# Six norms between blocks: the end of one block and the beginning of the next run by token block, and the norm weight is multiplied in before the transpose

## The reference

```
for l in 0, 1:
    h  = rms_norm(x, g_mix[l])                  # norm "mix", l
    x += merged(branches(h @ w_in[l])) @ w_merge[l]
    h2 = rms_norm(x, g_ffn[l])                  # norm "ffn", l
    x += (silu(conv3(h2 @ w_gate[l])) * (h2 @ w_up[l])) @ w_down[l]
for l in 0, 1:
    h  = rms_norm(x, norm_w_2[l])               # norm "two", l
    x += concat(mla, gated delta rule, block attention)(h @ w_in_2[l]) @ w_out_2[l]
out = rms_norm(x, final_norm_w_2)

rms_norm(x, g) = x * rsqrt(mean(x * x) + 1e-6) * g      # over the 1024 channels
```

## Time and profile before

| | |
|---|---|
| median of 3 runs | 1332.8 us (1332.27 to 1333.74) |
| the profiled execution | 1334.22 us, span of the profile 1332.4 us |
| PE busy | 98% of the span, granted clock 0.995 of full |
| DVE, ACT, POOL busy | 77%, 56%, 4% |
| DMA | 223.62 MB, mean 168 GB/s |

### The profile page before, as it was taken

The page is one execution under the profiler, slowest core; times in us unless marked ns, Lnnn a source line. Parts: engine busy times, 40 slices in busy tenths (PEclk is TensorE's granted clock), DMA queues, the critical chain, the costliest instruction groups (busy, mean ns, idle before and its releaser), DMA issues. The chain is left out here.

```text
span 1332.4 us, 26404 instructions
## 1 busy us (share of the span) xinstructions
PE 1302.1 (98%) x10796; PEld 1240.9 (93%) x10796; DVE 1030.1 (77%) x1769; ACT 742.9 (56%) x1143; POOL 47.3 (4%) x48
## 2 busy tenths in 40 slices
PE   8999999999999999999999999999999999999998
PEld 8899999999999999999999989999989899888997
DVE  6999998677777677999997768777778846677565
ACT  6554566556455465543746556444567445585363
POOL 0000000000000000000000000000001100001100
PEclk9999999999999999999999999999999999999999
DMA  8565455465555465656355554655654223433231
GB/s 280 187 206 175 157 173 175 160 222 177 203 190 190 152 228 179 212 164 202 126 198 164 192 188 169 213 200 195 205 161 151 65 97 127 131 132 111 81 102 74
DMA packets 108991, 223.62 MB, mean 168 GB/s; under 512 B 6180, under 2 KB 17700, under 8 KB 108872
## 3 DMA queue, kind: packets, MB, share of 16 engines
q1 hardware_dynamic: 106736, 218.99, 49.3%
q10 hardware_dynamic: 2136, 2.96, 0.7%
HBM read 220.88 MB, written 1.06 MB: 167 GB/s over the span
## 5 line engine op out<-in xcount | busy, mean ns | idle before, releaser
L1191 ACT ACTIVATE whi<-ring 128x1024 fp32r<-128x1024 f32 (+3 forms) x430 | 433.2, 1026 | 343.6 <-PE bank L513 218.2
L1766 DVE TENSOR_TENSOR wlo<-ring,whi 128x1024 fp32r<-128x1024 f32 (+3 forms) x430 | 497.4, 1181 | 164.0 <-ACT whi L1191 136.8
L513 PE MATMUL bank<-hhi,whi 128*128 128x256 f32 x2016 | 273.4, 278 | 4.3 <-ACT sgb L1442 1.8
L522 PE MATMUL bank<-hhi,wlo 128*128 128x256 f32 x2016 | 272.8, 277 | 1.0 <-DVE wlo L1766 1.0
L513 PE MATMUL bank<-hlo,whi 128*128 128x256 f32 x2016 | 270.4, 276 | 0.0
L513 PEld LDWEIGHTS bank<-hhi,whi 128*128 128x128 f32 x2016 | 249.2, 193 | 7.3 <-issue 4.0
L522 PEld LDWEIGHTS bank<-hhi,wlo 128*128 128x128 f32 x2016 | 246.8, 192 | 4.9 <-issue 3.2
L513 PEld LDWEIGHTS bank<-hlo,whi 128*128 128x128 f32 x2016 | 248.6, 194 | 0.0
L1946 DVE SCALAR_TENSOR_TENSOR w<-w,par 128x256 f32<-128x256 f32 x240 | 98.3, 486 | 0.0
L535 PE MATMUL bank<-whi,hhi 128*128 128x512 f32 (+2 forms) x256 | 93.1, 366 | 0.0
L535 PE MATMUL bank<-whi,hlo 128*128 128x512 f32 (+2 forms) x256 | 92.6, 364 | 0.0
(11 more groups left out here) (312 smaller groups left out, 1547.8 us busy)
## 6 DMA issues: line engine op xcount, KB each, us to landing
ring<-in_w_in SPq DMA_DIRECT2D x100, 1024.0 KB, 5.2
ring<-in_w_ffn_down SPq DMA_DIRECT2D x22, 1024.0 KB, 5.1
ring<-in_w_ffn_gate SPq DMA_DIRECT2D x20, 1024.0 KB, 5.2
ring<-in_w_ffn_up SPq DMA_DIRECT2D x20, 1024.0 KB, 5.1
ring<-in_w_merge SPq DMA_DIRECT2D x8, 1024.0 KB, 5.1
ring<-in_w_out SPq DMA_DIRECT2D x8, 1024.0 KB, 5.1
ring<-in_w_oc SPq DMA_DIRECT2D x4, 1024.0 KB, 5.9
ring<-in_w_od SPq DMA_DIRECT2D x4, 1024.0 KB, 5.2
```

Of the source, the lines that this page charges most:

```text
L513: done = e.matmul(o, wh[:, k, cols(u)], paired(s_[:, k0 + k, :]), stop=False, skip_group_check=True, start=opens and k == 0 and s_ is sh a ...
L522: done = e.matmul(o, wl[:, k, cols(u)], paired(sh[:, k0 + k, :]), start=False, stop=closes, skip_group_check=True)
L1191: e.activation(part_of(whi, j), part_raw(j), ACT.Copy).then_inc(*up("hi.a"))
L1766: e.tensor_tensor(part_of(wlo, j), part_raw(j), part_of(whi, j), ALU.subtract).then_inc(*up("lo.v"))
```

## The change

- `last_pairs` takes the last two row pairs (four parts) instead of one: all four for token block 0, then all four for token block 1. The transposes of token block 0 of the following norm stand before the last of these eight pieces.
- `chans_first` takes the first group of a block. Each of its four blocks of output channels has a bank of its own. A matmul of the high weights moves 128 tokens of `hhi` and the same 128 of `hlo` (256 columns, `hboth`), so a bank has the high and low products beside each other, by token block; token block 0 of all four parts is first, then the transposes of token block 1 (just before them the last half part of token block 0 is held back; in the first norm the transposes come first), then token block 1 and the low weights part by part. Moving operands here are not `paired`.
- The two sides of a bank are added when they are read: ACT copies one side, DVE adds the other (four copies and four additions, for glu_b, the first gate and kc).
- The norm weight multiplies `x` into `xn` before the scale and the transpose (`weigh`, from a broadcast row `rowg` that a 512 KB transfer on ACT's queue brings for each norm but the first), so `hhi` and `hlo` are written in four pieces of 512 columns each. The first norm keeps the weight behind the transposes, in pieces of 128 columns.
- Squares go to `sgb`; the `awake` matmuls of the norms go (13 stay at the start); glu_a, the first "up" and "ba" take "s" banks; the splits of the next block's first two parts move from the end of the old block into the norm.

```diff
-            def last_pair(j, acc, src, k0, tag, l):
+            def last_pairs(j, acc, pairs, tag, l, following):
+                for tb in range(2):
+                    for n, ((sh, sl), k0, ready) in enumerate(pairs):
+                        for nh in range(2):
+                            part = j + 2 * n + nh
...
+                            elif n == 1 and nh == 1 and following:
+                                turn_norm(*following, 0)
...
+            def chans_first(j, held_of, name, l, mid, after):
+                held = []
+                def products(i, tb, blocks_):
...
+                        for k in range(2):
+                            done = e.matmul(held[u][:, tb * S:tb * S + S], wh[:, k, cols(u)], hboth[:, :, 2 * i + k, cols(tb)],
+                                            start=i == 0 and k == 0 and tb == 0, stop=False, skip_group_check=True)
+                    return done
+                begins = name == "mix" and l == 0
+                if begins:
+                    turn_norm(name, l, 1)
+                for i in range(4):
+                    e.wait_ge(SEM["hi.a"], j + i + 1)
+                    e.wait_ge(*at("hlo", name, l, 0, i // 2))
+                    products(i, 0, (0, 1))
+                    if i == 3 and not begins:
+                        turn_norm(name, l, 1)
+                    products(i, 0, (2, 3))
+                for i in range(4):
+                    e.wait_ge(*at("hlo", name, l, 1, i // 2))
+                    products(i, 1, range(4)).then_inc(*up("first.p"))
+                    mid(j + i)()
+                    low_ready(j + i)
+                    wl = part_of(wlo, j + i)
+                    for u in range(4):
                         for k in range(2):
+                            done = e.matmul(sides(held[u])[0], wl[:, k, cols(u)], two(hhi[:, 2 * i + k, :]), start=False,
+                                            stop=i == 3, skip_group_check=True)
...
+            def norm_a(name, l, x_in, j0):
+                square_a(name, l, x_in, 0)
+                split_to(j0 + 2)
+                high_a(name, l, 0, 0)
+                high_a(name, l, 0, 1)
+                square_a(name, l, x_in, 1)
+                split_to(j0 + 3)
+                scale_a(name, l, xn)
+                high_a(name, l, 1, 0)
+                high_a(name, l, 1, 1)
...
+                for nh in range(2):
+                    add(0, nh)
+                    weigh(0, nh)
                 sums_v(name, l, 0)
+                for g in range(2):
+                    scale_v(name, l, 0, g, xn)
+                add(1, 0)
+                weigh(1, 0)
+                low_v(name, l, 0, 0)
+                add(1, 1)
+                low_v(name, l, 0, 1)
                 sums_v(name, l, 1)
+                weigh(1, 1)
+                scale_v(name, l, 1, 1, xn)
+                split_to(j0)
+                low_v(name, l, 1, 0)
+                split_to(j0 + 1)
+                low_v(name, l, 1, 1)
...
+                        if name == "kc":
+                            e.wait_ge(*at("z4", l))
+                            for c in range(4):
+                                e.activation(two(gdp[:, c // 2, c % 2, 3:259]), sides(bank(name, l, c))[0],
+                                             ACT.Copy).then_inc(*up("two.a"))
...
+                    if name == "kc":
+                        for c in range(4):
+                            g2 = two(gdp[:, c // 2, c % 2, 3:259])
+                            e.wait_ge(*at("kc_high", l, c))
+                            e.tensor_tensor(g2, g2, sides(bank(name, l, c))[1], ALU.add).then_inc(*up("two.v"))
```

More of the change, by code:

```diff
@@ L574, in norm_p, with turn_norm @@
[L574 to L588, removed]
+            def turn_norm(name, l, tb):
+                for g in range(2):
+                    bk = ps.take(e, "s", "nT", name, l, tb, g)
+                    e.wait_ge(DMA["id"], 16)
+                    e.wait_ge(*at("xn", name, l, tb, g))
+                    for i in range(4):
+                        done = turn(bk[:, cols(i)], xn[:, tb, cols(4 * g + i)])
+                    done.then_inc(*up("norm.p"))
+                    put("norm.p", "nT", name, l, tb, g)
@@ L758, in mix_p @@
                 for name, kind, n, _ in MIX_IN:
-                    held = [ps.take(e, "m", name, l, i) for i in range(2)]
+                    if name == "glu_b":
+                        chans_first(j, lambda u: ps.take(e, "m", name, l, u), "mix", l, between, behind)
+                        j += 4
+                        put("second.p", name, l)
+                        continue
+                    held = [ps.take(e, "s" if name == "glu_a" else "m", name, l, i) for i in range(2)]
                     for i in range(4):
[L761 to L764, removed]
+                        (chans if kind == "chans" else toks)(j, held, n, hh, 2 * i, i == 0, i == 3, between(j))
                         behind(j)
@@ new lines, in high_a @@
+            def high_a(name, l, tb, g):
+                bk = bank("nT", name, l, tb, g)
+                e.wait_ge(*at("nT", name, l, tb, g))
+                if name == "mix" and l == 0:
+                    for i in range(4):
+                        c = 4 * g + i
+                        e.activation(hhi[:, c, cols(tb)], bk[:, cols(i)], ACT.Copy,
+                                     scale=prm("g_mix", l, c, c + 1)).then_inc(*up("norm.a"))
+                else:
+                    e.activation(hhi[:, 4 * g:4 * g + 4, cols(tb)], heads(bk[:, :]), ACT.Copy).then_inc(*up("norm.a"))
+                put("norm.a", "hhi", name, l, tb, g)
@@ new lines, in low_v @@
+            def low_v(name, l, tb, g):
+                bk = bank("nT", name, l, tb, g)
+                e.wait_ge(*at("hhi", name, l, tb, g))
+                if name == "mix" and l == 0:
+                    for i in range(4):
+                        c = 4 * g + i
+                        e.scalar_tensor_tensor(out=hlo[:, c, cols(tb)], in0=bk[:, cols(i)], scalar=prm("g_mix", l, c, c + 1),
+                                               in1=hhi[:, c, cols(tb)], op0=ALU.mult, op1=ALU.subtract).then_inc(*up("norm.v"))
+                else:
+                    e.tensor_tensor(hlo[:, 4 * g:4 * g + 4, cols(tb)], heads(bk[:, :]), hhi[:, 4 * g:4 * g + 4, cols(tb)],
+                                    ALU.subtract).then_inc(*up("norm.v"))
+                leave("norm.v", "nT", name, l, tb, g)
+                put("norm.v", "hlo", name, l, tb, g)
```

369 lines of the change are left out of this document (207 added, 162 removed).

## The result

Timed beside the kernel before, on one chip and in turns, the changed kernel took **1338.52 us** (median of 5, 1337.65 to 1339.81) against 1332.27 (5 runs): ratio 1.0052, 95% interval 1.0041 to 1.0064. It is slower by 5.5 to 8.5 us. The forecast was 1335.8, range 1328 to 1344.

A forecast was written before the change was run, and what follows sets the result against it. PE, busy 98% of the span, was taken as the bound, so only its waits or idle work could be won. Terms +1.5 - 3.6 + 3.0 + 2.3 - 0.2 + 0 = +3.0 on 1332.8 gave 1335.8, range 1328 to 1344.

The forecast's parts named there:

- Boundary, -1.2 each: Norms ffn 0, mix 1, ffn 1: stretch 24.4 against 25.6, 1.2 won each, 3.6 for three.
- Weight supply: At the boundaries, SP's load three ahead waits for low halves and leaves at t = 18.3 instead of 6.9.
- "Two", l=0, +3.0: First "two" boundary: 3.0 us lost through the late load, with bias-table transfers in the same 10 us.
- upper bound of 4.5: Loss at "two", l=0, if DMA costs 3 us and more at each "two" boundary.
- "Two", l=1, +2.3: Second "two" boundary: qc 2.2 later through the late load, plus about 0.1 for the later ba copy.
- the 1.4 for the fuller wire: "Two", l=1: transfer of parts 7 and 8 lands 1.4 later, at t = 28.1 instead of 26.7.
- Start, +1.5: Kernel start until glu_a: 24.6 against 23.1, +1.5 (0 to +3), with ACT as the chain.
- Plain reading, 0: 576 first-group matmuls not read in pairs: taken as no cost, bounds -3 to +60.
- The late load does not decide in two: "Two" boundaries: late load harmless, all five boundaries give 1.2; total 1328.1, chance 0.28.
- Nothing much: Whole kernel: late load harmless for DMA, copies and additions in "two" at the lower bound; +1.1, 1333.9, chance 0.25.
- the landing unmoved: "Two" boundaries' lower bound: copies, additions and the later ba copy alone cost 1.5 and 1.9.
- Plain reading is slow: First-group matmuls: +60 (1396) at plain fp32 pace, +6.5 (1342) at a tenth more; chance 0.10.

The follow-up runs named there:

- experiment 11: New layout kept at ffn 0, mix 1, ffn 1 and end, paired first groups, tables early; old start order and 'two' boundaries: 1327.74 us, 0.9962 to the kernel before.
- Experiment 1: Changed kernel with the five bias-table transfers moved from the beginning of "two" to the FFN of block 1: 1335.74 us, 1.0030 to the kernel before.
- experiment 3: Changed kernel with the next block's first two low halves written before the addition of bank 2, in "two" norms only: 1334.91 us, 1.0025 to the kernel before.
- 6: Changed kernel with bias tables sent early and, in the "two" norms, low halves written early: 1331.75 us, 1.0003 to the kernel before.
- Experiment 10: Changed kernel with tables and low halves early, weight row late, paired first groups, and the start ordered as before: 1331.97 us, 1.0000 to the kernel before.
- Experiment 8: The kernel before with every moving operand of `chans` read plainly instead of in pairs: 1344.33 us, 1.0098 to the unedited kernel before.
- 5: Changed kernel with bias tables sent early and the weight row's transfer issued at vc, 30 us later: 1334.33 us, 1.0020 to the kernel before.
- after: The changed kernel itself, without further edits, against the kernel before: 1338.52 us, ratio 1.0052.
- 7: Changed kernel with bias tables early, low halves early in the "two" norms, and weight row issued at vc: 1331.84 us, 1.0006 to the kernel before.

## Why the prediction was right, and where its sum was not

The direction and the mechanism held: boundaries shorter, "two" longer through the late ring load. Point by point:

- *Boundary, -1.2 each.* 24.43, 24.42 and 24.42: 1.2 less each. The predicted cause holds as well (small waits for DVE's and ACT's pieces, 0.51 the largest), and experiment 11 kept the gain with "two" left alone.
- *Weight supply.* Predicted to leave at t = 18.3; it left at 18.2.
- *"Two", l=0, +3.0: the step that failed.* It was +7.49, and above the upper bound of 4.5. The prediction counted the bias tables only as more transfers in the same 10 us, which make the ring load late. They are themselves waited for: PE's bias matmuls are issued inside the kc group, and the flip matrix came 8.7 us after its issue. The side work that PE runs inside a group was not in the list of what waits for DMA, nor was it seen that before the matrix landed just in time, so that PE coming 2.3 earlier was itself lost. Experiment 1 takes the tables away (-2.8 at the median), 3 the late load (-3.6), 6 both (-6.8): this term and the one of l=1 together.
- *"Two", l=1, +2.3.* Right in kind, too large in size. The wait at qc grew from 0.70 to 2.77, but counted from the start of the boundary qc is only 0.9 later (t = 30.0, before 29.1), where 2.2 was predicted. The chain behind the transfer of parts 7 and 8 is as worked out: 3.1 from its landing to qc (predicted 3.2). The landing is not: ACT gets that transfer at t = 26.9 (1171.34 - 1144.43) where 28.1 was predicted and 26.7 stood before, so the 1.4 for the fuller wire was 0.2. A part of it was never there: the norm's row is sent behind a norm for the next one, and behind the norm of l=1 none is sent. Then the gate's wait of 1.28 and rows8's of 0.40 were gone, since their chains were no longer late against PE. More clock was lost ahead of the comparison point after (0.69 over 1170 to 1180) than before. The sum is +0.16 by the table; how much of it each took was not measured singly. Nor is the row firm: the trace of experiment 1, with the same code in l=1, has +1.6 for it, and one fall of the clock more or less is 1.7.
- *Start, +1.5.* +1.03, right in kind. A further 0.52 came at 115 us, where PE waits longer for a low half. Experiment 10 brings the start back and not this wait (1.56): it has another cause, left open.
- *Plain reading, 0.* It costs 0.013 per eight, 0.9 us in all. It hides in the other rows of the table; of the bounds given, -3 to +60, the sign of the low end was wrong. There the prediction set the trace against the Trainium skill (SBUF — State Buffer, the remark on cachelines), by which paired reading would be the slow one. Experiment 8 shows the opposite on PE's moving operand, and the measurement decides: plain 0.906 for eight, paired 0.893.
- *Rivals.* "The late load does not decide in two" is excluded by 3 and 6. "Nothing much" is wrong for l=0; its premise, the landing unmoved, nearly held in l=1 (0.2). "Plain reading is slow" is true in sign, at a sixth of the price given for its lower case.

The missed terms have both signs: -0.5 at the start, +0.5 at 115 us, +4.5 in l=0, -2.1 in l=1, +2.4 together. So 1335.8 was only 2.7 low because two errors in "two" offset each other in part. That is luck: the sum was closer than its largest term.

## What to carry to other kernels

When a step that is moved also moves a DMA issue, list every consumer of every transfer in that stretch, the side work's too, and not only the stream's own: here 64 KB for four small products set the time. A boundary that is laid out anew should be priced place by place, since the same edit gained 1.2 at three places and lost 7.5 at a fourth; keeping it at the three was worth more than any repair at the fourth. A gain in waits under an engine that is 97% busy shows in the start times of one instruction in both traces, long before a median can tell it.

## What the runs showed of the hardware

- A matmul of 256 columns with an fp32r moving operand read in pairs (columns 128 or 64 apart side by side) took 0.112 us (0.893 for eight); read plainly 0.113 (0.906 for eight), in some stretches 0.118 (0.94): +12.7 us for 6816.
- Transfers of 64 and 128 KB took 8.7 and 7.6 us from issue to landing when 1 MB of weights and the norm's row left just before them and the rate then stood at 380 to 400 GB/s; 5.2 and 5.0 with the row but not that load (experiment 3); 3.6 and 3.7 with neither (the kernel before).
- The granted clock fell between its two levels (2.4 and 1.2 GHz) during PE's wait of 7.40 (984.36 to 991.76): 1.00 over 985 to 989, then 0.56 and 0.59 over the next two windows of 4 us, 1.00 behind them.
- With the same code at the start and the same wait of PE ahead of the second transposes (1.55), the clock over 9 to 13 us was 1.00 in three traces (experiments 3, 5, 6) and 0.58 to 0.61 in three others (after, 1, 7).
